# Feed-forwards of a two-part transformer: down projection of nine blocks by seven products of sums, gate and up by token tile in one bank

## The chip, the cores and the metric

The kernel runs on one core of one Trainium2 chip. The metric is the device time of one launch in microseconds (us); less is better. A core has five engines with instruction queues of their own, which run in order and wait for each other by semaphores: PE (TensorE, matrix products into PSUM), DVE (VectorE), ACT (ScalarE), POOL (GpSimd) and SP (SyncE, which here only issues DMAs).

## The reference

Two blocks of two layers each run one after the other on one sequence of 256 tokens with 1024 features, all in float32. Between mixers of four kinds stand eight feed-forwards, with 2816 hidden features each, and only these are changed:

```python
D_MODEL = 1024; BATCH = 1; SEQ = 256; DEPTH = 2; D_FF = 2816

def swiglu(x, w_gate, w_up, w_down):
    return (jax.nn.silu(x @ w_gate) * (x @ w_up)) @ w_down

def first_block(...):
    ...
    for layer in range(DEPTH):
        h = h + 0.5 * swiglu(rms_norm(h, norm_ffn[layer, 0]), ...)
        hn = rms_norm(h, norm_mix[layer])
        ...                                   # pool/fox mixer, or MLA mixer
        h = h + 0.5 * swiglu(rms_norm(h, norm_ffn[layer, 1]), ...)
    return rms_norm(h, norm_final)
```

The second block does the same with `swiglu_2`, whose gate and up weights are the halves of one matrix, and with an mLSTM and a sparse attention mixer.

## The kernel before, in words

**Precision.** Every float32 operand of a product is split into a high part, rounded to the matrix format fp32r, and a low part, the difference. `mm3` then takes three matmuls for each product: high by high, high by low, low by high. ACT writes the high part (`prepare_hi`, line 492), DVE subtracts for the low part (`prepare_lo`, line 501). Both do this for every weight, as tiles of 128 partitions by 1024 elements: raw weights land by DMA in `raw`, the parts go to `wh` and `wl`, and, for every second block's down weights, to `mh` and `ml`, so that the down weights have two places.

**Blocks.** The 2816 hidden features of a feed-forward are cut into 11 blocks of 256. One PSUM bank holds 128 x 512 values, and there are eight: `A0` to `A3`, `G0`, `G1`, `X0`, `X1`. For block b, `gate_up(b, half)` multiplies both token tiles (128 tokens each) by half of the input features' rows of 256 gate and 256 up columns: 24 matmuls for each half, 48 in all, into two banks (`G0`, `G1` for even b, `X0`, `X1` for odd). `down(b - 1)` then multiplies the hidden values of the block before by its 256 x 1024 down weights: 2 token tiles x 2 halves of the 256 features x 2 halves of the 1024 columns = 8 products, 24 matmuls, which add up in `A0` to `A3` over all blocks. A step of PE is thus 72 matmuls of 512 columns.

**Between gate/up and down** lies a chain over three engines: ACT's silu (line 1815), DVE's product with up (`hidden`, line 2491), DVE's transposition in squares of 32 x 32 (`turn_squares`, line 2497), copies of the squares to their places, 8 by ACT (line 1832) and 8 by POOL (line 805), ACT's high part (`hid_hi`, line 1838) and DVE's low part (`hid_lo`, line 2502). The last block of a feed-forward is turned by PE instead (`turn_last_hid`, line 987). The residual (`residual_bank`, line 2402) multiplies the four banks by half the normalizing factor of the row and adds them to `h`.

**What sets the order.** The order on each engine is written out by hand, as `step(b)` of each engine, with a loop over steps 3 to 8. A weight place is given back by PE through the semaphores `used`; the gate/up places are there once for each half. SP issues each block's three loads of 1 MB as soon as the low parts of two blocks earlier are done. POOL does nothing in a feed-forward but the 8 copies of each block; `small_loads`, eight small DMAs issued from POOL, follow behind the first feed-forward.

## Time and profile before

| | us |
|---|---|
| median of 3 runs (lowest, highest) | 1938.38 (1938.18, 1938.87) |
| profiled execution, its time | 1938.43 |
| profiled execution, span of its core | 1936.5 |
| PE busy | 1922.3 (99%) |
| DVE busy | 1189.8 (61%) |
| ACT busy | 1190.5 (61%) |
| POOL busy | 392.5 (20%) |

The span is that of the trace; the execution takes 1.93 us more. A line such as `L501` is line 501 of the kernel; `out<-in` names the tiles. PE's matmuls overlap: each shows about 0.39 us, and they start about 0.227 us apart, so a matmul's cost is read from distances between starts. Where an instruction waits for something inside its engine, its duration contains that wait.

### The profile page before, as it was taken

To read this page: it belongs to the slowest core of one execution; us is meant where nothing else is said; L and a number is where in the kernel's file an instruction comes from. 1 tells how busy PE (TensorE), PEld (TensorE's weight loads), DVE (VectorE), ACT (ScalarE), POOL (GpSimd) and SP (SyncE) were. 2 spreads that over 40 slices of the span, in tenths; PEclk is the share of its full clock that TensorE was granted. 3 is DMA by queue.
4 is the path that set the end of the run, shared out by engine and by line. 5 is a ranking of instruction groups with operands and counts; after the bars stand their busy time and mean duration, and the time that the engine had idled before them with its cause. 6 is when DMAs were issued, how large, how long until landed. Compare 5 with 4: busy or idle time off the path is not lost.

```text
span 1936.5 us, 26905 instructions
## 1 busy us (share of the span) xinstructions
PE 1922.3 (99%) x9518; PEld 1621.1 (84%) x9518; DVE 1189.8 (61%) x1641; ACT 1190.5 (61%) x2147; POOL 392.5 (20%) x717
## 2 busy tenths in 40 slices
PE   9999999999999999999999999999999999999999
PEld 7888988888888898888888898888888888888887
DVE  6655656556655666555755666755576555877554
ACT  7555557555655666555755547755577555766553
POOL 1222302221222002221222100222112221211221
PEclk9999999999999999999999999999999999999999
DMA  9657436564655426665555434655556553306550
GB/s 326 211 189 216 153 110 203 191 194 150 225 191 184 142 76 218 196 195 174 192 193 193 161 131 142 206 195 195 174 172 226 191 194 130 109 21 217 198 195 23
DMA packets 241056, 338.96 MB, mean 175 GB/s; under 512 B 5727, under 2 KB 206350, under 8 KB 240830
## 3 DMA queue, kind: packets, MB, share of 16 engines
q1 hardware_dynamic: 239710, 335.84, 52.8%
q0 software_dynamic: 496, 1.23, 0.3%
q8 instruction: 58, 0.95, 0.2%
q10 hardware_dynamic: 752, 0.61, 0.1%
q14 instruction: 40, 0.33, 0.1%
HBM read 336.61 MB, written 1.05 MB: 174 GB/s over the span
## 4 chain that ended last, share of the span: by engine, by line
PE 94%; DVE 2%; ACT 2%; DMA 1%; issue 1%; POOL 0%; SPq 0%; ACTq 0%; DVEq 0%
PE A L540 11%; PE A L542 11%; PE A L541 11%; PE G L540 10%; PE G L542 10%; PE G L541 10%; PE X L540 8%; PE X L542 8%; PE X L541 8%; PE A L1247 1%; PE A L925 1%; PE X L1231 1%; DVE wl L501 1%; PE G L1259 1%; ACT wh L492 0%
## 5 line engine op out<-in xcount | busy, mean ns | idle before, releaser
L501 DVE TENSOR_TENSOR wl<-raw,wh 128x1024 fp32r<-128x1024 f32 (+1 forms) x553 | 658.4, 1231 | 134.5 <-ACT wh L492 133.6
L492 ACT ACTIVATE wh<-raw 128x1024 fp32r<-128x1024 f32 (+1 forms) x553 | 555.9, 1052 | 179.3 <-PE G L542 73.4
L805 POOL COPY work<-work 32x128 f32<-32x128 f32 x640 | 323.6, 506 | 909.9 <-DVE work L2497 886.6
L540 PE MATMUL G<-wh,xh 128*128 128x512 f32 (+1 forms) x814 | 317.9, 391 | 0.9 <-ACT arena L2267 0.7
L542 PE MATMUL G<-wh,xl 128*128 128x512 f32 (+1 forms) x814 | 316.3, 389 | 0.0
L541 PE MATMUL G<-wl,xh 128*128 128x512 f32 (+1 forms) x814 | 316.1, 388 | 0.0
L540 PE MATMUL X<-wh,xh 128*128 128x512 f32 x672 | 261.7, 389 | 1.1 <-DVE wl L501 1.1
L542 PE MATMUL X<-wh,xl 128*128 128x512 f32 x672 | 261.5, 389 | 0.0
L541 PE MATMUL X<-wl,xh 128*128 128x512 f32 x672 | 261.4, 389 | 0.0
L1832 ACT ACTIVATE work<-work 32x128 f32<-32x128 f32 x640 | 196.5, 307 | 16.1 <-DVE work L2497 9.6
L2502 DVE TENSOR_TENSOR hidl<-work,hidh 128x512 fp32r<-128x512 f32 x80 | 55.4, 692 | 237.8 <-ACT hidh L1838 237.8
L540 PEld LDWEIGHTS G<-wh,xh 128*128 128x128 f32 x814 | 152.8, 188 | 33.2 <-ACT arena L2267 0.8
L542 PEld LDWEIGHTS G<-wh,xl 128*128 128x128 f32 x814 | 152.8, 188 | 31.5
L541 PEld LDWEIGHTS G<-wl,xh 128*128 128x128 f32 x814 | 152.8, 188 | 30.9
L540 PE MATMUL A<-wh,hidh 128*128 128x512 f32 x384 | 150.2, 391 | 0.9 <-DVE hidl L2502 0.8
L541 PE MATMUL A<-wl,hidh 128*128 128x512 f32 x384 | 149.5, 389 | 0.0
L542 PE MATMUL A<-wh,hidl 128*128 128x512 f32 x384 | 149.5, 389 | 0.0
L540 PEld LDWEIGHTS X<-wh,xh 128*128 128x128 f32 x672 | 126.1, 188 | 27.9 <-issue 1.9
L542 PEld LDWEIGHTS X<-wh,xl 128*128 128x128 f32 x672 | 126.1, 188 | 26.3
L541 PEld LDWEIGHTS X<-wl,xh 128*128 128x128 f32 x672 | 126.1, 188 | 26.2
L1838 ACT ACTIVATE hidh<-work 128x512 fp32r<-128x512 f32 x80 | 50.6, 632 | 125.9 <-POOL work L805 125.9
L1815 ACT ACTIVATE work<-G,st 128x256 f32<-128x256 f32 x96 | 40.4, 472 | 141.9 <-PE G L542 141.0
(486 smaller groups left out, 2949.9 us busy)
## 6 DMA issues: line engine op xcount, KB each, us to landing
raw<-in_ffn_w_in SPq DMA_DIRECT2D x88, 1024.0 KB, 6.8
raw<-in_ffn_w_down SPq DMA_DIRECT2D x44, 1024.0 KB, 5.0
raw<-in_ffn_w_out SPq DMA_DIRECT2D x44, 1024.0 KB, 4.9
raw<-in_ffn_w_gate SPq DMA_DIRECT2D x42, 1024.0 KB, 5.5
raw<-in_ffn_w_up SPq DMA_DIRECT2D x42, 1024.0 KB, 7.3
raw<-in_a_w_in SPq DMA_DIRECT2D x12, 1024.0 KB, 5.3
...
```

The source lines that it names most:

```text
L492: nc.scalar.activation(hi, r, ACT.Copy).then_inc(hi_done[u], 1)
L501: nc.vector.tensor_tensor(lo, r, hi.bitcast(F32), ALU.subtract).then_inc(lo_done[u], 1)
L540: nc.tensor.matmul(o, sh, rh, start=start, stop=False)
L541: nc.tensor.matmul(o, sh, rl, start=False, stop=False)
L542: return nc.tensor.matmul(o, sl, rh, start=False, stop=stop)
L805: last = nc.gpsimd.tensor_copy(*square_views(i, j))
L925: last = nc.tensor.transpose(NB[b][:, i * S + t * P:i * S + (t + 1) * P], h[:, t, c * P:(c + 1) * P], ident)
L1231: last = nc.tensor.transpose(X[n % 2][:, i * P:(i + 1) * P], probs[:, n % 2, i * P:(i + 1) * P], ident)
L1815: A_(silu[:, t, :], GB[b % 2][t][:, 0:S], ACT.Silu, scale=rstd[:, t:t + 1]).then_inc(silu_ready, 1)
L1832: last = A_(*square_views(i, j), ACT.Copy)
L1838: A_(hidh[:, b % 2, :], hid_t, ACT.Copy).then_inc(hidh_done, 2)
L2502: V.tensor_tensor(hidl[:, b % 2, :], hid_t, hidh[:, b % 2, :].bitcast(F32), ALU.subtract).then_inc(hidl_done, 2)
```

## The change

**Seven products.** In blocks 0 to 8 of each feed-forward (`SEVENS` = 9) the down product of 2 x 2 tiles by 2 x 2 tiles is formed by Winograd's form of Strassen's rule: seven products instead of eight, four sums of weight tiles (128 x 512) and four sums of hidden tiles (128 x 128) ahead of them. The seven products stay in seven banks over the nine blocks: `A0` to `A3`, `G1`, `X0`, `X1`. Only behind block 8 are the banks combined (`first_sum`, `bank_parts` on DVE) and added to `h` (`add_sums` on POOL). Blocks 9 and 10 keep the eight products.

**Who forms the sums.** POOL: `weight_sums` before its 8 copies of a block, `hidden_sums` behind them. The high and low parts (`seven_hi`, `seven_lo`, `hid_hi`, `hid_lo`) now cover 3584 elements of each partition for a block's down weights and 896 for its hidden values, where they covered 2048 and 512. The down parts have one place instead of two.

**Gate and up by token tile.** With seven banks taken, one is left. From block 2 on `gate_up(b, t)` takes one token tile over all input features, 24 matmuls, in bank `G0`, and the second tile may overwrite it only when DVE has read the first. A weight half is given back in the second tile, and the first tile needs both halves. PE's step is `gate_up(b, 0)`, `seven_last(b - 2)` (3 products, 9 matmuls), `gate_up(b, 1)`, `seven_first(b - 1)` (4 products, 12 matmuls): 69 matmuls.

**The ends.** The last block's hidden values are turned by DVE, ACT and copies (`last_squares`, `last_moves`) and no longer by PE. Half the normalizing factor is multiplied in `hidden`. The down weights of block 0 are loaded behind block 1's gate and up weights. `small_loads` moves on POOL into block 4 of the first feed-forward.

```diff
+        hid_sums = cut(arena, 4864, 3 * P)
+        w_sums, bank_sums = cut(yf, 0, 3, 512), [cut(yf, at, 512) for at in (1536, 0, 512, 1024)]
...
+            def weight_sums(f, b):
+                G_, block = nc.gpsimd, T0[f"ffn{f}"] // 2 + b
+                at = lambda k: sums_of(f, b, k)
+                w = raw_view(block, 2)
+                b11, b12, b21, b22 = w[:, 0, 0:512], w[:, 0, 512:D], w[:, 1, 0:512], w[:, 1, 512:D]
+                t1, t2, t3 = (w_sums[:, k, :] for k in range(3))
+                pool.wait_ge(raw_landed[block % 2][2], landing[block, 2])
+                if b:
+                    pool.wait_ge(lo_done[2], n_of[2 * block - 1, 2])
+                summed(G_.tensor_tensor(t1, b12, b11, ALU.subtract), at(1))
+                summed(G_.tensor_tensor(t3, b22, b12, ALU.subtract), at(2))
+                pool.wait_ge(pool_summed, at(1))
+                summed(G_.tensor_tensor(t2, b22, t1, ALU.subtract), at(3))
+                pool.wait_ge(pool_summed, at(3))
+                summed(G_.tensor_tensor(b12, b21, t2, ALU.subtract), at(4))
             def move_squares(f, b):
                 n = 2 * (FFN_BLOCKS * f + b) + 2
                 if b:
                     pool.wait_ge(hidl_done, n - 2)
+                pool.wait_ge(pool_summed, sums_of(f, b, 4 if b < SEVENS else 0))
                 pool.wait_ge(hid_turned, n)
                 for i in (2, 3):
                     for j in range(4):
                         last = nc.gpsimd.tensor_copy(*square_views(i, j))
                 last.then_inc(hid_moved, 1)
...
+            def hidden_sums(f, b):
...
+                pool.wait_ge(hid_moved, 2 * ((FFN_BLOCKS + 1) * f + b) + 2)
+                summed(G_.tensor_tensor(s1, a21, a22, ALU.add), at(1))
+                summed(G_.tensor_tensor(s3, a11, a21, ALU.subtract), at(2))
+                pool.wait_ge(pool_summed, at(1))
+                summed(G_.tensor_tensor(s2, s1, a11, ALU.subtract), at(3))
+                pool.wait_ge(pool_summed, at(3))
+                summed(G_.tensor_tensor(a21, a12, s2, ALU.subtract), at(4))
...
+            def add_sums(f):
...
+                pool.wait_ge(hid_moved, 2 * ((FFN_BLOCKS + 1) * f + SEVENS) + 2)
+                for k, (t, n, part, count) in enumerate(((0, 0, 0, 1), (1, 0, 2, 3), (0, 1, 3, 4), (1, 1, 1, 5))):
+                    pool.wait_ge(part_sums, 5 * f + count)
+                    col = h[:, t, 512 * n:512 * (n + 1)]
+                    summed(nc.gpsimd.tensor_tensor(col, col, bank_sums[part], ALU.add), sums_of(f, SEVENS, k + 1))
...
             def ffn(name):
                 f = int(name[3:])
-                for b in range(FFN_BLOCKS - 1):
+                for b in range(SEVENS):
+                    weight_sums(f, b)
+                    if f == 0 and b == 4:
+                        small_loads()
                     move_squares(f, b)
+                    hidden_sums(f, b)
+                move_squares(f, SEVENS)
+                add_sums(f)
...
+                def gate_up(b, t, turn=None):
...
+                    bank = X[t] if b == 1 else G[0]
+                    if b > 1:
+                        pe.wait_ge(hid_done, 2 * (FFN_BLOCKS * f + b) + t + at)
+                    for half in (0, 1):
+                        if t == 0:
+                            for u in (0, 1):
+                                pe.wait_ge(lo_done[u], n_of[tile + half, u] + at)
+                        for i, c in enumerate(CHUNKS[4 * half:4 * half + 4]):
+                            col = slice(256 * (c % 4), 256 * (c % 4 + 1))
+                            last = mm3(bank[:, :], xh[:, c, tok], xl[:, c, tok], wh[:, half, 0:2, col], wl[:, half, 0:2, col],
+                                       half == 0 and i == 0, half == 1 and i == 3)
+                        if t == 1:
+                            last.then_inc(used[1], 1)
+                    if t == 0:
+                        last.then_inc(first_done, 1)
...
+                def seven_first(b, turn=None):
...
+                    pe.wait_ge(lo_done[2], n_of[base + 2 * b, 2] + 2 * at)
+                    pe.wait_ge(hidl_done, 2 * (FFN_BLOCKS * f + b) + 1 + at)
+                    ah, al = hid_hi_parts, hid_lo_parts
+                    bh, bl = down_parts(0)
+                    for bank, i, j in ((3, 2, 0), (0, 3, 2), (1, 0, 3), (2, 1, 1)):
+                        part = slice(P * i, P * (i + 1))
+                        last = mm3(A[bank][:, :], ah[:, part], al[:, part], bh[:, j, :], bl[:, j, :], b == 0,
+                                   b == SEVENS - 1 and bank == 3)
+                    last.then_inc(used[2], 1)
...
+                def seven_last(b, turn=None):
...
+                    if b == 0:
+                        pe.wait_ge(hid_done, 2 * (FFN_BLOCKS * f + 1) + 2)
+                    pe.wait_ge(lo_done[2], n_of[base + 2 * b + 1, 2] + 2 * at)
+                    pe.wait_ge(hidl_done, 2 * (FFN_BLOCKS * f + b) + 2 + at)
+                    ah, al = hid_hi_parts, hid_lo_parts
+                    bh, bl = down_parts(1)
+                    for k, bank in enumerate((G[1], X[0], X[1])):
+                        part = slice(P * (4 + k), P * (5 + k))
+                        last = mm3(bank[:, :], ah[:, part], al[:, part], bh[:, k // 2, k % 2, :], bl[:, k // 2, k % 2, :],
+                                   b == 0, b == SEVENS - 1)
+                    last.then_inc(used[2], 1)
...
+                def step(b, turn=None):
+                    gate_up(b, 0, turn)
+                    seven_last(b - 2, turn)
+                    gate_up(b, 1, turn)
+                    seven_first(b - 1, turn)
...
-                def step(b, turn=None):
-                    gate_up(b, 0, turn)
-                    gate_up(b, 1, turn)
-                    down(b - 1, turn)
...
                 gate_up(end, 0)
+                seven_last(SEVENS - 1)
                 gate_up(end, 1)
-                wait_down(end - 1)
+                pe.wait_ge(lo_done[2], n_of[base + 2 * SEVENS + 1, 2])
+                pe.wait_ge(hidl_done, 2 * (FFN_BLOCKS * f + SEVENS) + 2)
+                pe.wait_ge(part_sums, 5 * f + 1)
+                for q, i in enumerate(RES):
+                    for j in range(2):
+                        last = down_part(SEVENS, i, j)
+                        if q == 3:
+                            last.then_inc(used[2], 1)
+                pe.wait_ge(part_sums, 5 * f + 5)
...
                 for q, i in enumerate(RES):
-                    if q == 3:
-                        turn_last_hid()
-                    for j in range(2):
...
+                    if q < 2:
+                        pe.wait_ge(hidl_done, 2 * (FFN_BLOCKS * f + end) + q + 1)
...
+                        act.wait_ge(used[2], done_at[base + 2 * b - 1, 2][1] + at)
+                    A_(hid_hi_parts[:, 2 * S:7 * P], hid_sums, ACT.Copy).then_inc(hidh_done, 1)
...
+                def step(b, turn=None, split=()):
...
-                    gate(b - 1, turn)
-                    for half in downs:
-                        prep(name, half, (2,))
+                    if b == 1:
+                        gate(0, 0)
+                    gate(b - 1, 1, turn)
                     for u in (0, 1):
                         if (1, u) not in split:
                             prepare_hi(base + 2 * b + 1, u, turn)
                     move_squares(b - 1, turn)
-                    hid_hi(b - 1, turn)
+                    if b <= SEVENS:
+                        seven_hi(b - 1, 0, turn)
+                        gate(b, 0, turn)
+                        hid_hi(b - 1, turn)
+                        seven_hi(b - 1, 1, turn)
+                        return
+                    prep(name, 2 * SEVENS, (2,))
+                    prep(name, 2 * SEVENS + 1, (2,))
+                    gate(b, 0)
+                    whole_hid_hi(SEVENS)
+                    last_moves(0)
+                    last_hid_hi(0)
                     for half in (0, 1):
-                        prepare_hi(base + 2 * b + half, 2, turn)
+                        prep(name, 2 * b + half, (2,))
+                    prep(name, FT, (0, 1))
+                    gate(b, 1)
+                    last_moves(1)
+                    last_hid_hi(1)
...
+                def first_sum():
+                    dve.wait_ge(used[2], done_at[base + 2 * SEVENS - 2, 2][1])
+                    V.tensor_copy(bank_sums[0], A[3][:, :]).then_inc(part_sums, 1)
...
+                def bank_parts():
+                    dve.wait_ge(used[2], done_at[base + 2 * SEVENS - 1, 2][1])
+                    for o, bank, add, n in ((1, X[0], 0, 1), (2, X[1], 1, 2), (3, G[1], 1, 2), (1, G[1], 2, 4)):
+                        dve.wait_ge(part_sums, 5 * f + n)
+                        V.tensor_tensor(bank_sums[o], bank[:, :], bank_sums[add], ALU.add).then_inc(part_sums, 1)
...
+                def step(b, turn=None, split=()):
...
-                    hidden(b - 1, turn)
+                    if b == 1:
+                        hidden(0, 0)
+                    hidden(b - 1, 1, turn)
                     turn_squares(b - 1, turn)
-                    for half in downs:
-                        prep(name, half, (2,))
                     for u in (0, 1):
                         if (1, u) not in split:
                             prepare_lo(base + 2 * b + 1, u, turn)
-                    hid_lo(b - 1, turn)
+                    if b <= SEVENS:
+                        seven_lo(b - 1, 0, turn)
+                        hidden(b, 0, turn)
+                        hid_lo(b - 1, turn)
+                        seven_lo(b - 1, 1, turn)
+                        return
+                    first_sum()
+                    prep(name, 2 * SEVENS, (2,))
+                    prep(name, 2 * SEVENS + 1, (2,))
+                    hidden(b, 0)
+                    whole_hid_lo(SEVENS)
+                    last_squares(0)
+                    last_moves(0)
+                    last_hid_lo(0)
+                    bank_parts()
                     for half in (0, 1):
-                        prepare_lo(base + 2 * b + half, 2, turn)
+                        prep(name, 2 * b + half, (2,))
+                    prep(name, FT, (0, 1))
+                    hidden(b, 1)
+                    last_squares(1)
+                    last_moves(1)
+                    last_hid_lo(1)
```

**POOL, the first feed-forward behind its first block**, one whole block. Of before, the squares' copies alone:

```order
L805 COPY work<-work 32x4x32 [waits hid_turned,hidl_done]
L805 COPY work<-work 32x4x32 x7
L805 COPY work<-work 32x4x32 [waits hid_turned,hidl_done]
L805 COPY work<-work 32x4x32 x7
L805 COPY work<-work 32x4x32 [waits hid_turned,hidl_done]
```

Of after, where `y` holds the weight sums and `arena` the hidden sums:

```order
L863 TENSOR_TENSOR y<-raw 128x512 [waits lo2_done,raw12_landed]
L864 TENSOR_TENSOR y<-raw 128x512
L866 TENSOR_TENSOR y<-raw,y 128x512 [waits pool_summed]
L868 TENSOR_TENSOR raw<-raw,y 128x512 [waits pool_summed]
L879 COPY work<-work 32x4x32 [waits hid_turned,pool_summed,hidl_done]
L879 COPY work<-work 32x4x32 x7
L889 TENSOR_TENSOR arena<-work 128x128 [waits hid_moved]
L890 TENSOR_TENSOR arena<-work 128x128
L892 TENSOR_TENSOR arena<-arena,work 128x128 [waits pool_summed]
L894 TENSOR_TENSOR work<-work,arena 128x128 [waits pool_summed]
```

Four sums of 512 elements now stand ahead of the copies and four of 128 behind them; the first waits for `lo2_done`, DVE's last low part of the down weights of the block before.

**DVE, step 2 of a feed-forward.** Before:

```order
L501 TENSOR_TENSOR wl<-raw,wh 128x1024 [waits hi0_done]
L501 TENSOR_TENSOR wl<-raw,wh 128x1024 [waits hi1_done]
L2491 TENSOR_TENSOR work<-X,work 128x256 [waits silu_ready] x2
L2497 STREAM_TRANSPOSE work<-work 128x512 [waits hid_done]
L501 TENSOR_TENSOR wl<-raw,wh 128x1024 [waits hi0_done]
L501 TENSOR_TENSOR wl<-raw,wh 128x1024 [waits hi1_done]
L2502 TENSOR_TENSOR hidl<-work,hidh 128x512 [waits hidh_done]
L501 TENSOR_TENSOR wl<-raw,wh 128x1024 [waits hi2_done] x2
```

After:

```order
L536 TENSOR_TENSOR wl<-raw,wh 128x1024 [waits hi0_done]
L536 TENSOR_TENSOR wl<-raw,wh 128x1024 [waits hi1_done]
L2656 SCALAR_TENSOR_TENSOR work<-X,st,work 128x256 [waits silu_ready]
L2663 STREAM_TRANSPOSE work<-work 128x512 [waits hid_done]
L536 TENSOR_TENSOR wl<-raw,wh 128x1024 [waits hi0_done]
L536 TENSOR_TENSOR wl<-raw,wh 128x1024 [waits hi1_done]
L2706 TENSOR_TENSOR ml<-raw,mh 128x1024 [waits hi2_done] x2
L2656 SCALAR_TENSOR_TENSOR work<-G,st,work 128x256 [waits silu_ready]
L2683 TENSOR_TENSOR hidl<-work,hidh 128x512 [waits hidh_done]
L2683 TENSOR_TENSOR hidl<-arena,hidh 128x384 [waits hidh_done]
L2706 TENSOR_TENSOR wl<-y,wh 128x1024 [waits hi2_done]
L2706 TENSOR_TENSOR wl<-y,wh 128x512 [waits hi2_done]
```

Two subtractions for the down weights became four (one of them of half size), the hidden values' one became two, and the two `hidden` products of a block are now parted.

## Rows read from the trace of the kernel before

**Rows 1.** The page: busy us, share of the span and instructions of each engine.
```profile
PE 1922.3 (99%) x9518; PEld 1621.1 (84%) x9518; DVE 1189.8 (61%) x1641; ACT 1190.5 (61%) x2147; POOL 392.5 (20%) x717
```

**Rows 2.** Busy time by stretch, 60 to 160 us: length, PE, PEld, DVE, ACT, POOL, clock, DMA.
```profile
60.00:160.00 100.00, 100.00 (x443) 82.81 (x442) 56.36 (x62) 58.91 (x104) 24.30 (x48) 1.00 0.63 200
```

**Rows 3.** Timeline of PE (start, length, instruction): ends of one `down` of 24 matmuls.
```profile
66.11 0.39 PE L540 MATMUL A<-wh,hidh 128*128 128x512 f32 x1
...
71.55 0.39 PE L540 MATMUL G<-wh,xh 128*128 128x512 f32 x1
```

**Rows 4.** Groups by shape, DVE and ACT: count, busy us, mean ns, idle before, releaser.
```profile
L501 DVE TENSOR_TENSOR wl<-raw,wh 128x1024 fp32r<-128x1024 f32 x549 | 654.5, 1232 | 131.4 <-ACT wh L492 130.5
L2497 DVE STREAM_TRANSPOSE work<-work 128x512 f32<-128x512 f32 x80 | 56.9, 711 | 8.8 <-DVE work L2491 0.5
L2491 DVE TENSOR_TENSOR work<-G,work 128x256 f32<-128x256 f32 x96 | 37.9, 424 | 104.7 <-ACT work L1815 104.6
L492 ACT ACTIVATE wh<-raw 128x1024 fp32r<-128x1024 f32 x549 | 552.5, 1053 | 177.6 <-PE G L542 71.7 <-PE X L542 66.5 <-PE A L542 36.4
L1815 ACT ACTIVATE work<-G,st 128x256 f32<-128x256 f32 x96 | 40.4, 472 | 141.9 <-PE G L542 141.0 <-POOL st L790 0.9
```

**Rows 5.** Groups by shape, POOL: the copies, sums of 512 and 256, two DMA issues.
```profile
L805 POOL COPY work<-work 32x128 f32<-32x128 f32 x640 | 323.6, 506 | 909.9 <-DVE work L2497 886.6
L898 POOL TENSOR_TENSOR arena<-arena,st 128x512 f32<-128x512 f32 x6 | 6.1, 1041 | 0.2
L879 POOL TENSOR_TENSOR arena<-arena,st 128x256 f32<-128x256 f32 x4 | 2.5, 616 | 37.0 <-DVE st L3122 37.0
L778 POOL DMA_DIRECT2D arena<-in_ab_w_in x1 | 1.1, 1131 | 0.0
L781 POOL DMA_DIRECT2D st<-in_a_b_if x1 | 0.5, 544 | 0.0
```

**Rows 6.** Timeline, pairs back to back: ACT's high parts, copies; DVE's low parts.
```profile
67.04 2.01 ACT L492 ACTIVATE wh<-raw 128x1024 fp32r<-128x1024 f32 x2
68.94 2.54 ACT L1832 ACTIVATE work<-work 32x128 f32<-32x128 f32 x8
...
74.61 2.36 DVE L501 TENSOR_TENSOR wl<-raw,wh 128x1024 fp32r<-128x1024 f32 x2 [0.19 <-ACT wh L492]
```

**Rows 7.** Timeline of DVE, POOL and ACT, 68 to 74 us, single instructions.
```profile
68.36 1.18 DVE L501 TENSOR_TENSOR wl<-raw,wh 128x1024 fp32r<-128x1024 f32 x1
69.73 1.19 POOL L805 COPY work<-work 32x128 f32<-32x128 f32 x1
70.96 1.94 POOL L805 COPY work<-work 32x128 f32<-32x128 f32 x6
73.00 0.63 ACT L1838 ACTIVATE hidh<-work 128x512 fp32r<-128x512 f32 x1 [1.52 <-POOL work L805]
73.73 0.69 DVE L2502 TENSOR_TENSOR hidl<-work,hidh 128x512 fp32r<-128x512 f32 x1 [2.96 <-ACT hidh L1838]
```

**Rows 8.** Timeline of DVE and POOL, 212 to 219 us (a mixer), single instructions.
```profile
212.76 1.80 DVE L501 TENSOR_TENSOR wl<-raw,wh 128x1024 fp32r<-128x1024 f32 x1
214.49 2.06 DVE L501 TENSOR_TENSOR wl<-raw,wh 128x1024 fp32r<-128x1024 f32 x1
216.47 1.75 DVE L501 TENSOR_TENSOR wl<-raw,wh 128x1024 fp32r<-128x1024 f32 x1
...
213.56 1.90 POOL L830 TENSOR_TENSOR arena<-arena 128x512 f32<-128x512 f32 x1
215.55 1.60 POOL L831 TENSOR_TENSOR arena<-arena 128x256 f32<-128x256 f32 x1
```

**Rows 9.** Timeline of PE: the last block's transpositions, start and length.
```profile
459.87 0.60 PE L987 MATMUL G<-const,work 128*128 128x128 f32 x4
```

**Rows 10.** Who waited for whom, PE: us in total, times, longest.
```profile
PE A L925 <- DMA h<-in_x: 1.7, 1, 1.7
...
PE X L540 <- DVE wl L501: 1.1, 2, 0.6
```

290 lines of the change are left out of this document (170 added, 120 removed).

## The prediction

> **What bounds the kernel now.** I read the page's busy times first. PE is busy for 99% of the span, DVE and ACT for 61%, POOL for 20% [rows 1]. Overlapping matmuls can look busy while they wait, so a stretch of feed-forward comes next: from 60 to 160 us PE shows 443 matmuls in 100 us at a granted clock of 1.00 (2.4 GHz) [rows 2], one in 0.226 us. The starts at both ends of one `down` are 5.44 us apart for 24 matmuls [rows 3], 0.2267 us each. The list of waits names hardly any of PE's: the two largest are 1.7 and 1.1 us in total [rows 10]. So PE issues without a gap and bounds the kernel; a step of 72 matmuls is 16.32 us. A matmul less is 0.227 us less, as long as the others keep up. What the others have is slack, and how it is used up decides this change.
>
> **What is saved.** Three matmuls in each of 9 blocks and 8 feed-forwards: 216 x 0.2267 = 49.0 us. The four transpositions of a last block span 0.60 us, and the last of them runs on into the next matmul [rows 9]; I take 0.44 us for each feed-forward (bounds 0 and 0.60), 3.5 us in all. Together 52.5 us, if PE never waits. PE's new step would be 69 x 0.2267 = 15.64 us.
>
> **What is added, engine by engine, for a block.** ACT: 1536 weight elements and 384 hidden ones for each partition more; 1024 cost 0.96 us back to back (2.01 for two, 1.053 for one) [rows 4, 6], so 1.9 us more. DVE: the same elements at 1.14 us for 1024 (2.36 for two, less 1.23) [rows 4, 6], about 2.3 us more, which makes some 11.3 us of a step. POOL: four sums of 512 at 1.04 us, and four of 128, for which no row stands; 256 take 0.616 and 512 take 1.041 [rows 5], 0.0017 us for an element, so 0.40 us (bounds 0.2 and 0.6). With 8 copies at 0.33 us (six in 1.94) [rows 7] POOL has 4.2 + 2.6 + 1.7 = 8.5 us and the hand-overs. Each alone fits into 15.64 us.
>
> **They are not alone.** This is the step that decides. When DVE subtracts two operands in SBUF and POOL reads SBUF at the same time, each waits for the other. In the mixer at 212 us three subtractions that take 1.23 us elsewhere take 1.80, 2.06 and 1.75, and POOL's sums of 512 and 256 take 1.90 and 1.60 in place of about 1.04 and 0.62 [rows 4, 5, 8]. The ends tell the order: DVE ends at 214.56, POOL at 215.46, DVE at 216.55, POOL at 217.15, DVE at 218.22 [rows 8]. They alternate, never together: behind DVE's end a sum of 512 needs 0.90 us, one of 256 0.60, and behind POOL's end a DVE subtraction of 1024 needs 1.08. In the feed-forward a copy that meets a subtraction takes 1.19 instead of 0.3 us [rows 7].  Before, POOL brought only 8 short copies; DVE hardly noticed them.
>
> **A steady step, walked through.** The chain that closes on itself is POOL sums, copies, hidden sums, ACT's high parts, DVE's low parts, POOL sums. Take as 0 the time when DVE has finished `seven_lo(b-1, 1)` and POOL starts its weight sums. DVE has then just begun its first subtraction for the next gate/up half (it ends at 1.0).
> - Weight sums: t1 ends at 1.9, DVE's second at 3.0, t3 at 3.9; t2 runs beside the hidden product (one operand in PSUM) and the transposition, which I take not to collide, 5.0; DVE's third ends at 6.05, t4 at 6.95. Uncontended it would be 4.3.
> - DVE's fourth ends at 8.0. ACT's high parts from the sums start at 7.05, so `seven_lo(b, 0)` follows at 8.2 to 9.4 and to 10.6. POOL's copies start at 7.0 and pass one at each end of those three, the last five at 0.33: 12.4. Uncontended 2.7 us, here 5.4.
> - Hidden sums: 4 x 0.40 and two waits for itself, 14.3.
> - ACT: hand-over 0.1 [rows 7], 512 and 384 elements at 0.53 and 0.42, then 1024 in 1.05: 16.4. DVE: 1.14, then 0.69 for 512 [rows 6, 7], hand-over to POOL 0.13: 18.4.
>
> So the step is about **18.4 us**, not 15.64. The same chain without mutual waiting is 13.1 us, under PE's 15.64. PE shows the difference as two waits in each step: about 2.0 us ahead of the second half of `gate_up(b, 0)`, whose low parts come as DVE's third and fourth, and 0.8 us ahead of its first half, where `hidden(b-1, 1)` has to free the bank.
>
> Bounds: with sums of 512 at 0.9 or 1.2 us the step becomes 17.7 or 19.1; sums of 128 at 0.3 or 0.5 give 18.0 or 18.8; if DVE's transposition waits for POOL too, 18.8.
>
> The Trainium skill (GPSIMD Engine Reference, section 3.1) gives 4497 ns for an addition of two tensors of 2048 float32 elements on GpSimd. By that, as an estimate, 512 elements are 1.12 us and the step 18.7. The row's 1.04 is used.
>
> **Start and end of a feed-forward**, carried through by the same durations.
> - Step 1: `gate_up(1, 0)` needs the second weight half 2.72 us after its place is free, but two silus (0.47), two high parts, two hidden products (0.42), a transposition (0.71) [rows 4] and two subtractions lie ahead: 4.8 us, so PE waits 2.1 us. In step 2 the chain above is already late: 4.5 us.
> - Steps 3 to 9: 7 x 2.76 = 19.3 us.
> - End: small waits in step 10 (0.4) and ahead of the last `down` (0.3). Behind `gate_up(10, 1)` DVE's queue holds four bank sums (0.69 each), two subtractions for block 10, lengthened by POOL's `add_sums`, and two of the next phase, before the last hidden product: it starts 7.9 us behind PE. Product, transposition of half size, 8 ACT copies (a full set is 2.54 [rows 6]; 2.2 taken, bounds 1.3 and 2.5), high part, low part: 12.1 us. PE has 5.4 + 1.4 of work and small waits until it needs them: it waits 5.1 us. The residual then stands behind two more subtractions: 1.4 us.
> - Sum of waits: 2.1 + 4.5 + 19.3 + 0.7 + 5.1 + 1.4 = 33.1 us, against 6.56 saved (27 matmuls and the transpositions): **+26.5 us** for each feed-forward, 212 us for eight. The last feed-forward has no next phase: -4 us.
> - `small_loads` now stands inside POOL's closed chain in the first one: eight issues between 0.54 and 1.13 us [rows 5], 6 us added.
>
> Moved loads: the down weights come later in SP's queue, but still about a step ahead of `weight_sums`; nothing is counted. Gate and up in one bank alone cost PE nothing: the same matmuls.
>
> 1938.4 + 212 - 4 + 6 = **2152 us**. The profiled execution (1938.43) and the median (1938.38) agree, so nothing is to be converted.
>
> **Rivals.**
> - *DVE and POOL do not hold each other up here* (weight sums read `raw` and `y`, the mixer's read `arena`). Then the step is 15.64 and only the ends wait: 2.0 + 3.2 + 1.4 = 6.6 us for each feed-forward, 53 us, against 52.5 saved: 1939 us. Against it: the waiting copies of rows 7 are in the feed-forward itself.
> - *The saving arrives.* The same, and DVE's short queue at the ends hides the turn: 1938.4 - 52.5 = 1886 us. It needs the second weight half within 2.72 us, which the sum of durations (4.8) doesn't allow.
> - *The pauses lower PE's clock.* No row of before shows a clock under 1.00; PE's longest wait is 1.7 us [rows 10], and now 5 us pauses come eight times. If the 12 to 48 matmuls behind each ran at half the clock, they would cost 2.7 to 10.9 us more: 22 to 87 us in all, 2174 to 2239 us. The Trainium skill (TensorE: Matmul & The Clock Gate, section "What's actually happening") says that an idle array is throttled from 2.4 to 1.2 GHz; no run here shows it.
> - *Only the weights' sums collide.* If the copies slip in at no cost, the chain is 2.7 us shorter than 18.4, 15.7; the weight sums still hold back DVE's gate/up subtractions, and with half of PE's waits left I take 16.9: 64 steps x 1.5 us and a little at the ends less, about 2040 us. Rows 7 speak against it.
>
> **How the numbers follow.** Forecast (18.4 us a step within its bounds, 2100 to 2200): 0.74. Clock: 0.10. Only the weights' sums: 0.06. No mutual waiting: 0.06. Saving arrives: 0.04. The step's bounds, 17.7 to 19.1, move 64 steps by 45 us either way, the end's copies by 7; with part of the clock's case the range is 2090 to 2215. A measurement of this kernel can tell 0.2%, 4 us, from no change. Slower holds the forecast, the clock, the weights' sums and half of the rest of no mutual waiting (0.92), same 0.03, faster 0.05.
>
> **What would show it.** PE's list of waits, before nearly empty, should name DVE's `wl` and `work` some 150 times, with 33 us in each feed-forward; steps 18.4 us apart; POOL busy most of the time, its 512 sums at 1.9 us in the mean of three of four, DVE's gate/up subtractions at 1.9 to 2.1. If these last are 1.23, the step on mutual waiting is wrong. If they are long but steps are 15.6 us apart, the closed chain is. If the granted clock falls under 1.00, the third rival is at work.

## The result, and the profile after

The changed kernel takes 2226.69 us (median of 4 runs, 2226.12 to 2227.27); the kernel before, on the same chip, 1938.38 us (median of three runs; a fourth took 5004.36 us and is left out). The ratio is 1.149, 95% interval 1.147 to 1.151. The forecast was 2152 us with a range of 2090 to 2215: the direction and the mechanism came as forecast, the size was 75 us too small, and the time lies 12 us outside the range.

The profiled execution spans 2225.5 us at a mean granted clock of 0.967, against 1936.5 us at 1.000. Its busy times and the clock in 40 slices, from the page:

```profile
PE 1976.7 (89%) x9270; PEld 1607.6 (72%) x9270; DVE 1634.2 (73%) x2041; ACT 1375.8 (62%) x2491; POOL 1206.7 (54%) x1325
...
PEclk9999999999899999999899999999999999999999
```

Against [rows 1], PE has 248 matmuls and transpositions less and is busy for 54 us more; its share of the span fell from 99% to 89%. POOL, at 20% before, now has 54%. The list of waits of PE (us in total, times, longest), against [rows 10]:

```profile
PE G L584 <- DVE wl L536: 95.5, 67, 2.2
PE G L584 <- DVE work L2656: 78.1, 73, 9.6
PE A L584 <- DVE hidl L2696: 38.9, 8, 5.4
PE X L584 <- DVE wl L536: 21.4, 8, 5.6
PE A L1024 <- DVE h L2569: 1.7, 2, 1.5
```

All waits of this list sum to 243.6 us, those of before to 10.8. They are at the forecast's places: the second half of `gate_up(b, 0)` (first line), the bank that a hidden product frees (second), the last hidden part of each feed-forward (third), step 1 (fourth). One stretch of feed-forward by engine (length, PE, PEld, DVE, ACT, POOL, clock, DMA share, GB/s), against [rows 2]:

```profile
360.00:460.00 100.00, 85.42 (x350) 66.78 (x349) 75.71 (x67) 61.06 (x106) 76.23 (x84) 0.97 0.50 161
```

350 matmuls in 100 us, where there were 443. The groups by shape (count, busy us, mean ns, idle before), against [rows 4, 5]:

```profile
L536 DVE TENSOR_TENSOR wl<-raw,wh 128x1024 fp32r<-128x1024 f32 x469 | 755.9, 1650 | 53.3 <-ACT wh L523 52.6
L2706 DVE TENSOR_TENSOR wl<-y,wh 128x1024 fp32r<-128x1024 f32 x72 | 88.2, 1225 | 14.9 <-ACT wh L1997 14.9
...
L864 POOL TENSOR_TENSOR y<-raw 128x512 f32<-128x512 f32 x72 | 156.2, 2170 | 0.0
...
L866 POOL TENSOR_TENSOR y<-raw,y 128x512 f32<-128x512 f32 x72 | 132.5, 1840 | 0.0
L863 POOL TENSOR_TENSOR y<-raw 128x512 f32<-128x512 f32 x72 | 132.2, 1836 | 260.0 <-DVE wl L2706 259.4 <-DMA raw<-in_ffn_w_down 0.5
```

The same subtraction of 1024 elements takes 1.225 us where POOL is idle (second line: behind the hidden sums). The subtractions of the first line, beside which POOL makes its weight sums, take 1.65 us on average over the whole run and 2.02 us from 360 to 460 us. The sums are longer too: 1.84 to 2.17 us. One meeting in detail, a steady step of the second feed-forward, single instructions of DVE and POOL (start, length):

```profile
412.98 2.32 DVE L536 TENSOR_TENSOR wl<-raw,wh 128x1024 fp32r<-128x1024 f32 x1
414.18 2.25 POOL L864 TENSOR_TENSOR y<-raw 128x512 f32<-128x512 f32 x1
...
415.22 0.47 DVE L2656 SCALAR_TENSOR_TENSOR work<-G,st,work 128x256 f32<-128x256 f32 x1
415.80 0.71 DVE L2663 STREAM_TRANSPOSE work<-work 128x512 f32<-128x512 f32 x1
...
416.40 1.29 POOL L866 TENSOR_TENSOR y<-raw,y 128x512 f32<-128x512 f32 x1
416.43 4.54 DVE L536 TENSOR_TENSOR wl<-raw,wh 128x1024 fp32r<-128x1024 f32 x2
```

DVE's subtraction ends at 415.30, POOL's sum 1.13 us behind it at 416.43: they alternate as in [rows 8]. `t2` runs undisturbed and takes 1.29 us, not the 1.04 that I took from [rows 5]. The next two subtractions take 2.27 us each beside it and `t4`. The transposition of DVE took its 0.71 us [rows 4] beside a sum.

**Where PE's time went.** 52.5 us of work are gone and 232.8 us of waits came (243.6 less 10.8); the span grew by 289.0. So 109 us more must be in PE's busy time. The mean clock says that for some 147 us (2 x 0.033 x 2225.5) the lower level was granted. About 19 us of these lie in the pauses, where PE does nothing; the other 128 us are about 64 us of delay. The rest is at the pauses themselves: the matmul ahead of a pause counts 0.39 us where the next would start 0.227 after it, and behind the first matmul after a pause the next one starts 0.31 us later. That is 0.25 us a pause, for some 165 pauses more than before about 41 us; together 105 of the 109. This is a balance of where PE's time stands, not of causes: what the half speed costs the kernel is a question for an experiment.

### The profile page after: what moved, and what is told of

Read it like the earlier page. It is cut to its first block and busy times, and to the rows that moved or that the text cites. A ratio compares the mean times of both kernels' runs of the same rounds, so it can differ in the third digit from the quotient of the medians.

```text
span 2225.5 us, 28336 instructions
## 1 busy us (share of the span) xinstructions
PE 1976.7 (89%) x9270; PEld 1607.6 (72%) x9270; DVE 1634.2 (73%) x2041; ACT 1375.8 (62%) x2491; POOL 1206.7 (54%) x1325
## 3 DMA queue, kind: packets, MB, share of 16 engines
q0 software_dynamic: 496, 1.23, 0.2%
HBM read 336.61 MB, written 1.05 MB: 152 GB/s over the span
## 5 line engine op out<-in xcount | busy, mean ns | idle before, releaser
L584 PE MATMUL G<-wh,xh 128*128 128x512 f32 (+1 forms) x1326 | 546.5, 412 | 175.5 <-DVE wl L536 95.5
L585 PE MATMUL G<-wl,xh 128*128 128x512 f32 (+1 forms) x1326 | 529.7, 399 | 0.0
L586 PE MATMUL G<-wh,xl 128*128 128x512 f32 (+1 forms) x1326 | 528.0, 398 | 0.0
L586 PEld LDWEIGHTS G<-wh,xl 128*128 128x128 f32 x1326 | 257.0, 194 | 56.5
L863 POOL TENSOR_TENSOR y<-raw 128x512 f32<-128x512 f32 x72 | 132.2, 1836 | 260.0 <-DVE wl L2706 259.4
L2706 DVE TENSOR_TENSOR ml<-raw,mh 128x1024 fp32r<-128x1024 f32 x144 | 178.1, 1277 | 69.9 <-ACT mh L1997 68.8
L1997 ACT ACTIVATE mh<-raw 128x1024 fp32r<-128x1024 f32 x144 | 144.6, 1051 | 57.5 <-POOL raw L868 56.8
L864 POOL TENSOR_TENSOR y<-raw 128x512 f32<-128x512 f32 x72 | 156.2, 2170 | 0.0
L868 POOL TENSOR_TENSOR raw<-raw,y 128x512 f32<-128x512 f32 x72 | 147.7, 2051 | 5.6
L2706 DVE TENSOR_TENSOR wl<-y,wh 128x1024 fp32r<-128x1024 f32 (+1 forms) x144 | 131.6, 955 | 14.9 <-ACT wh L1997 14.9
L584 PE MATMUL A<-mh,hidh 128*128 128x512 f32 x352 | 137.1, 390 | 0.9 <-DVE hidl L2683 0.9
```

The lines of the kernel that those rows point to most:

```text
L584: nc.tensor.matmul(o, sh, rh, start=start, stop=False)
L585: nc.tensor.matmul(o, sh, rl, start=False, stop=False)
L586: return nc.tensor.matmul(o, sl, rh, start=False, stop=stop)
L863: summed(G_.tensor_tensor(t1, b12, b11, ALU.subtract), at(1))
L864: summed(G_.tensor_tensor(t3, b22, b12, ALU.subtract), at(2))
L868: summed(G_.tensor_tensor(b12, b21, t2, ALU.subtract), at(4))
```

## The experiments

The theory: POOL's sums, copies, hidden sums, ACT's high parts and DVE's low parts close a chain that takes longer than PE's 69 matmuls, because DVE and POOL wait for each other. Rivals: DVE's own queue is full (D); POOL's own time, not the mutual waiting, fills the chain (P); the lowered clock is the cost (C). For every kernel I also read the **step**, the distance between the starts of `gate_up(b, 0)`: 64 of them, eight in each feed-forward. "Walk" is my walk along the chain, with POOL's sums at the 1.29 and 0.46 us of the trace after; for the changed kernel it gives 19.6, and 19.3 us is measured.

| Kernel | expected us | measured us | step expected | mean step |
|---|---|---|---|---|
| changed kernel | 2152 | 2226.7 | 18.4 | 19.31 |
| weight sums on 8 elements | 1993 | 1990.5 | 16.0 | 15.86 |
| hidden sums on 8 | 2150 | 2166.2 | 18.5 | 18.54 |
| both on 8 | 1959 | 1974.2 | 15.7 | 15.78 |
| weight sums on 256 | 2085 | 2074.4 | 17.4 | 17.06 |
| fills for weight sums | 2010 | 2009.4 | 16.2 | 16.15 |
| pauses filled | 2215 | 2231.9 | as changed | 19.31 |
| sums on DVE | 2098 | 2194.5 | 17.4 | 18.65 |
| the same, copies first | 2090 | 2100.4 | 17.2 | 17.54 |
| and hidden product first | 2055 | 2055.7 | 16.8 | 16.79 |

**Shorter sums.** The edit, on the weight sums (the hidden sums alike); the first of the four lines:

```diff
-                summed(G_.tensor_tensor(t1, b12, b11, ALU.subtract), at(1))
+                N = slice(0, 8)
+                summed(G_.tensor_tensor(t1[:, N], b12[:, N], b11[:, N], ALU.subtract), at(1))
```

> The four weight sums of POOL in each of the nine blocks work on 8 elements in place of 512; the down products then use unsummed weights, so the output is not the reference's. All instructions, waits and their order stay those of the changed kernel. Theory (closed chain): the step of the changed kernel (19.1 us at full clock) is the way from POOL's weight sums over the copies, the hidden sums, ACT's high parts and DVE's low parts back to POOL, and both the sums' own time and the lengthening of the DVE subtractions beside them lie on it. With the measured 1.29 us for a sum of 512 and 0.46 for one of 128 in my walk along the chain, a step without the long sums takes 16.0 us, little over PE's own 15.6; the time is about 1993 us (2226.7 - 233), between 1970 and 2020, and the DVE subtractions of the weights average about 1.25 us again in place of 1.65. Rival D (DVE's own queue, with more low parts than before, is the bound, and POOL merely runs beside it): the time stays at 2150 or more and the subtractions stay at about 1.6. Rival P (POOL's own time is the whole of it, nothing waits mutually): a step loses only the four sums, but the subtractions stay at 1.65 on average.

> The four hidden sums of POOL in each block work on 8 elements in place of 128 (the products use unsummed hidden parts, so the output is not the reference's); the rest is the changed kernel. Theory (closed chain): 4 x about 0.3 us and what they lengthen beside them leave a chain of 18.5 us a step at full clock; the time is about 2150 us (2120 to 2180), the wait of PE ahead of the second half of a gate and up (2.2 us) shrinks by about 0.6 us. Rival D (DVE's own queue is the bound): no change, 2226 within 0.3%. Rival W (the weight sums alone close the chain): no change either, since the hidden sums would have room.

> Both kinds of POOL's sums on 8 elements (weights and hidden parts unsummed in the products; output not the reference's). Theory (closed chain): the chain is shorter than PE's 69 matmuls, the step is PE's own 15.6 us, PE's pauses inside the steady steps are under 0.2 us, the clock is 1.0 through the steps, and what is left over before's time is the ends and starts of the eight feed-forwards: about 1959 us (1930 to 1985). If the ends and starts (some 13 us per feed-forward) stood alone, this is the number that shows them. Rival D (DVE's queue): 2150 or more. Rival C (the lowered clock is a lasting state that the seven-product order brings with it, whatever the pauses): the mean clock stays at 0.97 and half-clock stretches remain, about 2000 or more.

> POOL's weight sums on 256 elements in place of 512 (the other half of each sum is left out, and the products read unsummed weights, so the output is not the reference's). Theory (closed chain): a sum costs about 0.74 us in place of 1.29, the step 17.4 us at full clock, the time about 2085 us (2055 to 2115), that is a little over half of the way from the changed kernel to the kernel with short weight sums: the time follows the length of the sums. Rival L (what costs is that POOL and DVE meet at all, once per subtraction, whatever the length of the sum): about as slow as the changed kernel, 2190 or more. Rival D (DVE's queue): no change.

All four came within 17 us of what was expected. With short weight sums the subtractions are back (busy time and groups):

```profile
PE 1905.1 (96%) x9270; PEld 1595.2 (80%) x9270; DVE 1435.9 (72%) x2041; ACT 1377.8 (69%) x2491; POOL 886.5 (45%) x1325
...
L536 DVE TENSOR_TENSOR wl<-raw,wh 128x1024 fp32r<-128x1024 f32 (+1 forms) x473 | 580.3, 1266 | 52.5 <-ACT wh L523 51.6
```

DVE has every instruction it had and is busy for 198 us less. A full queue of its own (D) would have kept the time at 2150 or more. The 256-element sums put the time between the two (L falls), and the hidden sums count too, so the weight sums alone don't close the chain (W falls).

With both kinds short the steady steps are PE's own 15.64 us, and still the kernel is 1.8% slower than before (ratio 1.018, 1.016 to 1.021). Its waits of PE show what is left, at the ends and starts of the feed-forwards:

```profile
PE A L585 <- DVE hidl L2698: 32.0, 8, 4.5
PE X L585 <- DVE wl L536: 17.2, 8, 3.4
PE G L585 <- DVE work L2658: 6.9, 5, 3.3
```

All its waits are 65.0 us, 54 more than before's. Its mean clock is 0.982, by which the lower level was granted for 71 us; without the 9 us of these in pauses that is some 32 us of delay, and 20 pauses more at 0.25 us are 5. 54, 32 and 5 against 52.5 saved is about +38; measured is +36. So the seven products would not pay here even with sums that cost nearly nothing: as they stand, their ends and starts eat the saving.

**Fills in place of sums.**

```diff
-                summed(G_.tensor_tensor(t1, b12, b11, ALU.subtract), at(1))
+                summed(G_.memset(fill, 0.0), at(1))
+                pool.wait_ge(pool_summed, at(1))
```

> In place of each weight sum POOL fills 1408 elements per partition with zero (no operand is read), behind the same waits, with a wait for the one before between each two. In the trace of the kernel before, a fill of 1024 elements took 0.96 us, so 1408 should take about 1.3 us, as long as an undisturbed sum of 512. The sums are left out and the products read unsummed weights, so the output is not the reference's. It parts POOL's own time from the mutual waiting. Theory (closed chain through mutual waiting), if a fill does not collide with DVE: walked with 1.3 us for each and no lengthening a step is 16.2 us against 15.9 with short sums, so about 2010 us (1985 to 2035), DVE's weight subtractions at 1.27 us. Rival P (POOL's own 4 x 1.29 us on the chain is what costs, whoever runs beside it): 2130 or more. If fills collide with DVE as sums do, the time is about 2210 to 2230, the subtractions are at 1.6 us, and the run says nothing between the two.

```profile
L536 DVE TENSOR_TENSOR wl<-raw,wh 128x1024 fp32r<-128x1024 f32 x469 | 569.0, 1252 | 51.1 <-ACT wh L523 50.4
...
L865 POOL MEMSET y<- 128x1408 f32 x72 | 92.1, 1280 | 258.5 <-DVE wl L2709 258.1 <-DMA raw<-in_ffn_w_down 0.5
```

The fills take 1.28 us, as an undisturbed sum does, at the same places; no subtraction is lengthened, and the time is 2009.4 us. So 217 of the changed kernel's us (2226.7 less 2009.4) go when POOL is as long at work but reads nothing: that is what the mutual waiting of the weight sums costs. The fills in turn cost 19 us more than the sums of 8 elements (1990.5), two of which still meet DVE in most blocks (0.96 and 1.05 us on average). P falls. The Trainium skill (SBUF — State Buffer, "Who interferes with whom") says that a DVE instruction with two SBUF inputs contends with a GpSimd instruction that reads SBUF, not with one that only writes; the changed kernel and the one with fills agree on both halves, with 1.65 and 1.25 us for the subtraction.

**The collision in the kernel before.**

```diff
                 if b:
                     pool.wait_ge(hidl_done, n - 2)
+                    for k in range(4 if f < 4 else 0):
+                        nc.gpsimd.tensor_tensor(y[:, k // 2, 512 * (k % 2):512 * (k % 2 + 1)], h[:, 0, 0:512],
+                                                h[:, 1, 0:512], ALU.subtract).then_inc(pool_chain, 1)
+                        chain[0] += 1
+                        pool.wait_ge(pool_chain, chain[0])
```

> The kernel before, with four idle sums of 512 elements (h minus h into y, used by nobody) on POOL in each block from the second of the first four feed-forwards, ahead of its copies, each behind the end of the one before; the other four feed-forwards are as before, so one trace shows both. Theory: the collision belongs to the pair of instructions and not to the seven-product order: a sum takes about 1.3 us undisturbed and 1.8 to 2.3 beside a subtraction of DVE, and DVE's subtractions of 1024 (1.23 us) last 1.5 us or more on average in the four feed-forwards; the order of before has slack on DVE and POOL (PE waits 10.8 us in the whole run), so the time moves little: 1937 to 1965. Rival N (no mutual waiting; the long subtractions of the changed kernel come from its buffers or its order): sums at 1.04 to 1.3 us throughout, subtractions at 1.23, time within 0.2% of before. Rival D (DVE and POOL are already at their limit in the order before): each of the 40 steps grows by 2 us or more, 2010 or more.

It took 1960.55 us (ratio 1.012, 1.010 to 1.014). Its groups in a feed-forward with the sums, 360 to 460 us:

```profile
L501 DVE TENSOR_TENSOR wl<-raw,wh 128x1024 fp32r<-128x1024 f32 x30 | 55.1, 1882 | 0.6 <-ACT wh L492 0.6
...
L805 POOL TENSOR_TENSOR y<-h 128x512 f32<-128x512 f32 x24 | 46.6, 1941 | 11.0 <-DVE hidl L2507 9.6
```

and in one without them, 1300 to 1400 us:

```profile
L501 DVE TENSOR_TENSOR wl<-raw,wh 128x1024 fp32r<-128x1024 f32 x30 | 35.7, 1231 | 8.3 <-ACT wh L492 8.3
```

1.88 against 1.23 us: the collision belongs to the pair of instructions, not to the new order. And the order of before stands it; the stretch with the sums (columns as above):

```profile
360.00:460.00 100.00, 99.77 (x435) 80.80 (x434) 80.30 (x60) 57.81 (x102) 70.73 (x72) 1.00 0.59 189
```

Nothing there waits for the sums' results, only POOL's own copies stand behind them, and DVE at 80% still keeps up. What is fatal in the changed kernel is that the sums' results stand in the chain. Of its 23 us more, 10 are pauses of PE, mostly at the starts (3.4 us at 39 us, 4.9 at 524 us), and some 4 the half speed behind these two; the rest I can't place.

**The pauses filled.** Eight matmuls between the halves of `gate_up(b, 0)` and sixteen ahead of the last hidden part; the first of the two edits:

```diff
+                        if t == 0 and half == 1:
+                            col = slice(256 * (CHUNKS[3] % 4), 256 * (CHUNKS[3] % 4 + 1))
+                            for _ in range(8):
+                                mm(bank[:, :], xl[:, CHUNKS[3], tok], wl[:, 0, 0:2, col], start=False, stop=False)
```

> The changed kernel with PE's pauses filled: 8 more matmuls (low by low parts, 1.8 us) between the two halves of each gate and up of block 1 and later, where PE waits 2.2 us, and 16 more (3.6 us) ahead of the wait for the last hidden part, where PE waits 5.4 us. Theory (closed chain, PE not part of it): the chain neither shortens nor lengthens; the half-speed stretches, which begin within 2 us of a pause of 1.7 us or more, go away except at the starts, and what they cost is mostly hidden in the chain: 2215 us (2195 to 2235), mean clock 0.985 or more. Rival C (the lowered clock is a cost of its own, 37 stretches of 3.4 us at half speed, some 70 us in all): about 2160. Rival E (PE is the bound and its pauses are not real slack): 79 x 8 x 0.2267 and 8 x 16 x 0.2267 us come on top, 2350 or more.

It took 2231.94 us at a mean clock of 0.987 (768 matmuls more: the fill stands at 80 places, not the 79 that the expectation wrote).

```profile
die 0 (median of its cores): 2230.9 us, clock 0.987
...
PE G L584 <- DVE work L2665: 82.9, 70, 8.1
PE G L584 <- DVE wl L536: 11.9, 32, 0.6
```

174 us of added matmuls cost 5 us, and the stretches at half speed (those that hold three matmuls or more) went from 35 to 12, 13 of them fewer inside the steps, yet the mean step is 19.31 us, as without the fill. Inside the steps PE isn't in the chain: neither its pauses nor its clock cost anything there. C falls for the steps. For the ends and starts this run decides nothing: the stretches there went from 15 to 5, but the fill in blocks 1 and 10 and at the ends is work of its own there.

**The sums on DVE.** `weight_sums` moves from POOL's program to DVE's, with the same four operations:

```diff
+                        weight_sums(b - 1, turn)
                         seven_lo(b - 1, 0, turn)
                         hidden(b, 0, turn)
```

> The four weight sums of a block are done by DVE, ahead of its low part of the first down weights of that block, in place of POOL; the output is the reference's. Theory (closed chain): on DVE a sum of 512 should take about 0.6 to 0.7 us (half of the 1.23 us of its subtraction of 1024), nothing of POOL's runs beside the weight subtractions but copies and hidden sums, POOL is free; DVE has 2.6 us more a step. The walk gives 17.4 us a step, with a new wait of some 1.8 us, that of PE for the hidden part by token tile that stands behind the sums on DVE; about 2098 us (2060 to 2135), so faster than the changed kernel and still slower than the kernel before. Rival D (DVE's queue is already the bound): 4 x 0.65 us come on top of every step, 2226 + 72 x 2.6 = 2410. Rival L (the chain has slack behind POOL's copies): 2010 or less.

A miss, by 96 us. DVE's sums took 0.68 us each as expected, and the subtractions 1.25. POOL's row in a steady step names the error:

```profile
411.51 4.39 POOL L862 COPY work<-work 32x128 f32<-32x128 f32 x8 [12.27 <-DVE raw L2706]
```

POOL's copies waited for the last weight sum (DVE, 410.70 to 411.39), which they don't need: `move_squares` kept the wait that had only set the order of POOL's own work. The turned squares had been there since 406.6. The next two kernels move that wait behind the copies, and then DVE's hidden product ahead of its low parts:

```diff
-                pool.wait_ge(pool_summed, sums_of(f, b, 4 if b < SEVENS else 0))
+                if b == SEVENS:
+                    pool.wait_ge(pool_summed, sums_of(f, b, 0))
...
+                        hidden(b, 0, turn)
                         seven_lo(b - 1, 0, turn)
-                        hidden(b, 0, turn)
```

> The weight sums on DVE as in the kernel with sums on DVE (2194.5 us), but POOL's copies of the hidden parts no longer wait for these sums; only its hidden sums do. In the trace of that kernel the copies began at 411.5 us, right behind the last sum (411.39), though the turned squares were there at 406.62; my expectation of 2098 us had left that wait out, and walked with it a step comes out at 19.0 us against the 18.6 measured. Theory (the wait of POOL on the sums is what the miss consists of): a step of about 17.2 us, 2090 us (2065 to 2115), PE's wait at the hidden part 0.6 us shorter or gone at one of its two places. Rival D (DVE's queue is full with the sums, wherever POOL's copies stand): 2180 or more.

> As the kernel with the copies first, and on DVE the product that frees the gate bank of the next block stands ahead of the low parts of the first two weight parts of the down projection, not behind them. Theory: PE's wait of 1.5 to 1.8 us a step for that product goes, a new and smaller one comes at the low parts; the walk gives 16.8 us a step against 17.4, so 36 us less than the kernel with the copies first, about 2055 us (2030 to 2080). It stays slower than the kernel before: the ends and starts of the feed-forwards (about 60 us of waits and the half-speed stretches behind them) are untouched. Rival: the low parts are as urgent as the product, and the time stays within 10 us of the kernel with the copies first.

2100.4 and 2055.7 us: the second is 7.7% faster than the changed kernel, and still 6.1% slower than the kernel before (ratio 1.061, 1.059 to 1.063). In the second, PE's waits for the hidden products are 55.7 us where they were 101.2 in the first; at the ends 38.9 us stand as in the changed kernel. No version with seven products beats the kernel before.

**The saving alone.** The kernel before, with one of the eight products of `down` left out in nine blocks:

```diff
-                        for i in range(4):
+                        for i in range(j, 4):
```

> The kernel before with 69 matmuls in each of the nine blocks in place of 72: one of eight products of the down projection (three matmuls, first output part, second half) is left out, so the output is not the reference's. Nothing is added. It asks whether the saving itself is real, and what the order of before would give back. Theory: DVE, ACT and POOL of the kernel before have room for a step of 15.6 us, so 216 x 0.2267 = 49 us less, 1889 us (1885 to 1900), PE's waits still under 20 us and the clock at 1.0. Rival (the order of before is itself within 3% of its DVE and ACT limit, so that fewer matmuls turn into waits and lowered clock): 1915 or more.

```profile
PE 1873.7 (99%) x9302; PEld 1581.3 (84%) x9302; DVE 1189.4 (63%) x1641; ACT 1190.1 (63%) x2147; POOL 393.8 (21%) x717
```

1888.38 us, 48.8 less (ratio 0.975). The first term of the forecast, 216 x 0.2267 = 49.0 us, is right, and the order of before would have handed it on in full.

**The small loads.** Moved back behind the first feed-forward:

> The changed kernel with the small loads issued behind POOL's work of the first feed-forward, as in the kernel before, not in its fifth block. My prediction charged the move 6 us on POOL's path in that feed-forward. Theory (closed chain, POOL in it): 4 to 8 us less, 2220 us (2216 to 2224), and PE's wait of 3.4 us near 121 us gone. Rival: the loads lie beside other waits there, no change beyond 0.1%.

2225.96 us (2224.59 to 2227.03), against 2226.69: no difference that can be told. The wait of 3.4 us of PE at 121 us is gone, and other waits of that feed-forward are longer. My 6 us for it were wrong.

**Why a sum of 512 takes 1.29 us.** Three kernels: the sums with operands in two dimensions; the first two sums as one instruction of 1024; multiplications in place of subtractions.

```diff
+                two = lambda x: x.rearrange("p (n a) -> p a n", a=2)
...
+                G_.tensor_tensor(w_sums[:, 0:3:2, :], w[:, :, 512:D], w[:, 0, :].rearrange("p (a n) -> p a n", a=2),
+                                 ALU.subtract).then_inc(pool_summed, 2)
...
-                summed(G_.tensor_tensor(t1, b12, b11, ALU.subtract), at(1))
+                summed(G_.tensor_tensor(t1, b12, b11, ALU.mult), at(1))
```

> The changed kernel, with the operands of the four weight sums written as two dimensions (2 by 256, every second element) in place of one of 512; the same sums. In the trace of before a product of 512 with operands of several dimensions took 1.04 us; in the changed kernel the differences of 512 in one dimension take 1.29 us undisturbed. Theory S (it is the shape of the operands): 1.04 us undisturbed again, a step of 18.6 to 18.7 us in place of 19.2, about 2165 us (2150 to 2185), the length that my prediction had taken. Rival O (the operation or the operands' places decide, not the shape): 1.29 us undisturbed as before, 2226.7 within 0.3%. Rival T (a step of two elements costs POOL more): over 1.4 us and 2235 or more.

> The changed kernel, with the first two weight sums, b12 - b11 and b22 - b12, as one instruction of 1024 elements; the same sums. It has one dispatch and one meeting with DVE less. By the undisturbed 1.29 us for 512 and 0.46 for 128 (2.16 ns for an element, 0.18 us for an instruction) it should take 2.4 us undisturbed and the step 0.2 us less: about 2210 us (2200 to 2220). If the two-dimensional operands go at 1.66 ns for an element, 1.9 us undisturbed, a step 0.7 us shorter, about 2175 us (2160 to 2190). Rival: DVE now waits for a sum twice as long, and the time rises by 5 us or more.

> The changed kernel, with a multiplication in place of the subtraction in the four weight sums (same operands, shape and places; the output is not the reference's). The rows of before from which I took 1.04 us for 512 elements were products. Theory O (the operation decides): 1.04 us undisturbed, a step of about 18.4 us, 2165 us (2145 to 2185). Rival (a multiplication of these operands takes 1.29 us as the subtraction does; the rest of the difference lies in what the mixer's products read): 2226.7 within 0.3%.

Measured: 2288.3, 2219.6 and 2228.6 us. One row of each, in this order:

```profile
L865 POOL TENSOR_TENSOR y<-raw 128x512 f32<-128x512 f32 x72 | 172.5, 2396 | 0.0
```

```profile
L863 POOL TENSOR_TENSOR y<-raw 128x1024 f32<-128x1024 f32 x72 | 225.5, 3132 | 263.3 <-DVE wl L2707 261.5 <-DMA raw<-in_ffn_w_down 1.7
```

```profile
L864 POOL TENSOR_TENSOR y<-raw 128x512 f32<-128x512 f32 x72 | 156.1, 2169 | 0.0
```

Undisturbed, the sums took 1.48 to 1.51 us (two dimensions), 2.39 us (1024 elements) and 1.26 to 1.28 us (products), against 1.26 to 1.29 us for the differences of the changed kernel. The first is what its rival T expected, and its mean step is 20.14 us: 0.2 us more for each sum of 512 lengthen the step by 0.8 us, as a link of the chain should. One instruction for two sums takes the 2.4 us that two prices per element and one per instruction give, and saves 7 us, where 17 had been expected.

So neither the shape nor the operation explains the 1.04 us of [rows 5]. Two of POOL's sums in a mixer of the kernel before, which DVE's next subtraction (212.76 us, [rows 8]) meets only at the end of the second, are as quick:

```profile
210.04 1.89 POOL L828 TENSOR_TENSOR arena<-arena 128x1024 f32<-128x1024 f32 x1 [13.57 <-DVE arena L2668]
212.01 1.47 POOL L829 TENSOR_TENSOR arena<-arena 128x768 f32<-128x768 f32 x1
```

That is 1.65 ns for an element, as between the 256 and 512 of [rows 5]. By the kernel's text these add a tile to itself shifted by one or two elements, line 795 multiplies a tile by itself (1.04 us for 512), and line 898 multiplies by one value repeated over a whole head. All rows at 2.16 ns read two places that lie apart, also within one tile: the `h` minus `h` of the kernel before with sums took 1.29. What the quick ones have in common is thus that both operands are at the same or neighbouring elements, or one repeats its value; no run tests it, and the cause stays open.

## Why the forecast was right in kind and wrong in size

- *The saving*: right, 49 us (the kernel with 69 matmuls).
- *DVE and POOL wait for each other, read off [rows 7, 8]*: right, shown by the fills and by the added sums in the kernel before.
- *The chain that closes on itself*: right. The forecast's walk against the step from 412.07 to 431.23 us: weight sums 7.82 us, forecast 6.95; copies 5.39, forecast 5.45; hidden sums with their waits 1.92, forecast 1.9; ACT and DVE until POOL begins again 4.03, forecast 4.1. Three links of four are right within 0.1 us. **The step that failed is the price of POOL's sum of 512**: 1.04 us, from a row of the mixer whose second operand repeats one value; it is 1.29 undisturbed, and 1.13 in place of 0.90 behind DVE's end. By four sums that is the 0.87 us. The text's bound was 1.2 us for a sum, with a step of 19.1, so 19.2 without the one-off below lies a hair beyond it.
- The measured slope of these sums is (1.29 - 0.46) / 384 = 2.16 ns for an element. The Trainium skill (GPSIMD Engine Reference, section 3.1) has 4497 ns for an addition of 2048 elements. The measured slope agrees with the 2.2 ns for an element to which this comes; by it, as an estimate, the forecast's step is 18.7 us, nearer than the 18.4 by the row that the forecast used.
- *PE's two waits in a step*, 0.8 and 2.0 us: 1.1 and 1.4 on average (the first two lines of PE's waits). The second is 2.1 to 2.2 us in 24 places and 0.9 to 1.2 in 38. All waits are 30.5 us for each feed-forward where 33 had been forecast: half speed and the pauses' own cost fill the rest of the step. *Start and end*: 2.1 us forecast for step 1, 2.7 measured on average; 5.1 for the last hidden part, 4.9 measured; the residual's 1.4 us did not come (1.7 us for all eight).
- *The clock*: **a second term that the sum put at nothing**. The forecast held half speed behind pauses for a rival, with a chance of 0.10, as if it would come instead of the longer step. Only its upper bound took in a part. Half speed came together with the longer step, at a mean clock of 0.967. Here is a pause in a step and the matmuls behind it (start, length):

```profile
440.28 0.47 PE L584 MATMUL G<-wh,xh 128*128 128x512 f32 x1 [2.21 <-DVE wl L536]
440.58 0.39 PE L585 MATMUL G<-wl,xh 128*128 128x512 f32 x1
...
441.67 0.63 PE L586 MATMUL G<-wh,xl 128*128 128x512 f32 x1
442.10 0.63 PE L584 MATMUL G<-wh,xh 128*128 128x512 f32 x1
...
444.23 0.62 PE L586 MATMUL G<-wh,xl 128*128 128x512 f32 x1
444.66 0.43 PE L584 MATMUL G<-wh,hidh 128*128 128x512 f32 x1
```

  From 441.7 on they start 0.43 us apart, the lower of the two levels, for 8 matmuls, then 0.227 again. A step with such a stretch takes about 20.6 us and the next about 18, so the chain takes it back. At an end or a start, where PE itself is what all wait for, it should stay: 15 such stretches outside the steps, some 60 us long without the pauses in them, come to about 29 us. That half speed costs nothing inside the steps is shown by the filled pauses; the 29 us are counted from the clock and the matmuls' distances, and no run takes them away alone.
- *One-off*: in the third feed-forward PE waits 9.6 us once (the longest of the second row of its waits). DVE's `angles()` stands between steps 2 and 3, which was hidden while PE had work; that step takes 27.5 us, 8 more than the others.

The miss, summed: the 64 steps take 1236.0 us; the forecast had 8 x (20.1 + 7 x 18.4) = 1191. That is 45 us: 8 are `angles()`, and the other 37 are the price of the sums (64 x 0.87, about 56), less what the other links and the second step of each feed-forward had been charged too much. Outside the steps are the other 30 us, about the size of the half speed there. There the charges for the small loads and the residual, which were too high, stand against longer waits in step 1 and the pauses' own 0.25 us; that these cancel is luck. Neither the 45 nor the 30 us alone would have left the range; it took both.

Two slips in the forecast's sums change nothing: POOL's work for a block adds up to 8.4 us, not 8.5, and the chances for slower to 0.93, not 0.92.
